# Sliding attention in a two-layer decoder trunk: the scores of both key blocks packed into one 128x128 tile per head, turned once, and put back by masked copies on VectorE

## The chip, the cores and the metric

The kernel runs on one core of one Trainium2 chip. The metric is the device time in microseconds of one execution. The kernel before took 1579.21 us (median of 3 runs, 1577.72 to 1579.51).

## What is computed

Two layers of a hybrid decoder over 512 tokens and 1024 model columns, batch 1, float32. Each layer normalises x, makes one combined input projection and feeds three branches: a short gated convolution, a gated linear attention (GLA) and a sliding-window attention. Their outputs go through branch projections, gates and an output projection, and then through an MLP of width 4096. The part that matters here is the sliding attention: window 128, blocks of 128 queries, 8 query heads over 2 key heads of width 64, a sink per head.

```python
kw = with_prev_block(k)                          # the block before and this block: 256 keys
s = einsum('bnqkgd,bnckd->bkgnqc', qb, kw)
diff = qpos[:, :, None] - kpos[:, None, :]
mask = (diff >= 0) & (diff < SWA_WINDOW) & (kpos >= 0)
s = where(mask, s, -inf)
m = maximum(max(s, axis=-1), sink)
p = exp(s - m)
denom = sum(p, axis=-1) + exp(sink - m)
o = einsum('bkgnqc,bnckd->bnqkgd', p, vw) / denom
```

A query at place q of its block sees the keys 0 to q of its own block and the keys q+1 to 127 of the block before. So of the 256 columns of a score row exactly 128 count, and each column index 0 to 127 is valid in one of the two blocks, never in both. In the first block there is no block before.

## The kernel before, in words

All weights are streamed from HBM in units. For each unit ScalarE (ACT) writes a rounded high part (`split_high`, line 885), VectorE (DVE) the remainder (`split_low`, line 1193), and TensorE (PE) multiplies with three matmuls per 128x128 piece: high by high, low by high, high by low (lines 590 to 592, 612 to 614 and 653 to 655). Each matmul moves 512 columns. A unit is 24 of them; ACT and DVE split about three units ahead of PE. `+cx1` in a table of orders stands for the split of unit cx1; `cx1` on PE for its matmuls (`cx1.0` and `cx1.1` are the halves) and on DVE for reading its result out of PSUM.

Nothing is scheduled at run time. Three tables of words, `PE_ORDER`, `ACT_ORDER` and `DVE_ORDER`, say in which order each engine does the work of the first stage of a layer; each engine works strictly in its order, and semaphores make it wait for the others. Small products (scores, transposes, attention outputs) go through four PSUM banks that are used in turn: the n-th fill waits until fill n-4 has been read.

The sliding attention has eight steps per layer: i = 0 to 7, where i // 4 is the half of the heads (four heads each) and i % 4 the block of queries. For each i, in the code from line 785 on for PE, 1021 on for ACT and 1471 on for DVE:

- `SCi` on PE: scores of 4 heads in two banks, each 2 heads x 256 keys (only 128 keys where i % 4 is 0), line 790.
- `SCi` on DVE: per bank one add of the mask into `probs` (line 1479), then the maximum over all 4 heads (line 1483) and four small operations. `SCi` on ACT: one exp per head (line 1026). `SMi` on DVE: the reciprocal of the sum; `SMi` on ACT: the scaling per head (line 1033).
- `PTi` on PE: four transposes of 128x128 for the block before (`prev`) into one bank and four for the own block (`cur`) into another (line 801); where i % 4 is 0 only the latter. `PTi` on ACT: a copy of each bank into `probs_keys` (line 1039).
- `PVi` on PE: values times probabilities, for the block before and for the own block (line 809), which waits for the copies. `PVi` on ACT and DVE: high and low part of the result (lines 1046 and 1504).

Other words that the text needs: `KV` builds the GLA states on DVE (lines 1438 and 1443), `YG` scales the GLA outputs there (line 1463), `YT` turns and splits them (lines 780 and 1469), `cc`, `ct`, `cv`, `cl` are steps of the convolution, `GO` is the GLA output, `gate` the gates, `br` the branch projections.

```python
elif kind == "PV":
    ...
    if n:
        pe.wait_ge(pprev_ready, l * 6 + half * 3 + n)
        for kv in range(SWA_KV):
            weighted(kv, 0)
    pe.wait_ge(pcur_ready, l * 8 + i + 1)
```

Of the kernel before, what the change touches and what calls it, by code (L numbers as in the profile page):

```python
# [220 lines left out]
def hybrid_trunk(nc, x, x_cols, positions, params, w_in, gla_wa2, w_branch, w_o, w_up, w_down, norms, consts, gmask, out):  # L221
# [3 lines left out]
    with ctx:  # L225
# [330 lines left out]
        def _(pe):  # L556
# [1192 lines left out]
```

## Time and profile before

| what | value |
|---|---|
| median of 3 runs | 1579.21 us |
| the profiled execution's own time | 1577.71 us |
| its span, first to last instruction | 1575.9 us |
| PE busy | 1557.0 us, 99% of the span |
| DVE busy | 1040.5 us, 66% |
| ACT busy | 771.5 us, 49% |
| mean granted clock of TensorE | 0.999 of full speed |
| the sliding attention of layer 0 | from 102.5 us (SC0) to 229 us (PV7) |
| the sliding attention of layer 1 | from 884.7 us to 1012 us |

Times within the span are counted in microseconds from its start. The rows of PE give a matmul's duration from its issue to the end of its results (about 0.39 us for 512 columns), while the next one begins 0.23 us after it; what PE's time costs is therefore read from one start to the next, not from the durations.

### The profile page before, as it was taken

What the parts mean: (1) busy time and instruction counts of PE and PEld (TensorE: products, weight loads), DVE (VectorE), ACT (ScalarE), POOL (GpSimd) and SP (SyncE); (2) the same over time, 40 slices, a digit from 0 to 9 for tenths busy, and PEclk for the clock granted to TensorE, in tenths of its full rate; (3) what the DMA queues carried; (4) which work ended last, traced back from release to release, by engine and by line L of the source; (5) the groups of instructions that cost most, each with busy time, mean ns of one, the idle gap of its engine ahead of it and who ended that gap; (6) DMA issues with size and microseconds to landing.
All of it is one profiled execution on the core that took longest, in us unless ns stands there. A gap on an engine that the chain in (4) does not pass through costs nothing.

```text
span 1575.9 us, 21326 instructions
## 1 busy us (share of the span) xinstructions
PE 1557.0 (99%) x7488; PEld 1273.5 (81%) x7488; DVE 1040.5 (66%) x1487; ACT 771.5 (49%) x1163; POOL 106.9 (7%) x92
## 2 busy tenths in 40 slices
PE   8999999999999999999999999999999999999998
PEld 7877778888778888888787787788887888888886
DVE  5677664554776657586866777655457676665778
ACT  5657552222556464546445566432235563636362
POOL 0000000000121010111000000000002111101010
PEclk9999999999999999999999999999999999999999
DMA  7321314532596655748323212155316956666553
GB/s 236 103 81 57 95 64 147 173 107 81 131 222 140 176 138 150 172 109 208 56 84 104 82 54 81 54 172 175 107 54 151 243 115 178 143 174 135 142 125 94
DMA packets 132298, 201.48 MB, mean 128 GB/s; under 512 B 6592, under 2 KB 82912, under 8 KB 132192
## 3 DMA queue, kind: packets, MB, share of 16 engines
q1 hardware_dynamic: 107536, 153.36, 29.2%
q0 software_dynamic: 23936, 46.14, 17.6%
q8 instruction: 60, 0.98, 0.3%
q10 hardware_dynamic: 720, 0.61, 0.1%
q14 instruction: 46, 0.38, 0.1%
HBM read 170.74 MB, written 2.10 MB: 110 GB/s over the span
## 4 chain that ended last, share of the span: by engine, by line
PE 90%; DVE 6%; DVEq 1%; issue 1%; ACT 1%; DMA 0%; ACTq 0%
PE acc L590 19%; PE acc L592 19%; PE acc L591 19%; PE acc L653 6%; PE acc L655 6%; PE acc L654 6%; PE acc L612 3%; PE acc L614 3%; PE acc L613 3%; DVE wl_rows L1193 2%; DVE x_tokens L1555 1%; PE bank L790 1%; PE bank L809 1%; PE bank L801 1%; DVE ul L1212 1%
## 5 line engine op out<-in xcount | busy, mean ns | idle before, releaser
L590 PE MATMUL acc<-uh,wh 128*128 128x512 f32 x1152 | 452.8, 393 | 1.7 <-DVEq L1214 1.2
L592 PE MATMUL acc<-uh,wl 128*128 128x512 f32 x1152 | 448.7, 389 | 0.0
L591 PE MATMUL acc<-ul,wh 128*128 128x512 f32 x1152 | 448.5, 389 | 0.0
L590 PEld LDWEIGHTS acc<-uh,wh 128*128 128x128 f32 x1152 | 216.2, 188 | 54.0 <-issue 6.0
L592 PEld LDWEIGHTS acc<-uh,wl 128*128 128x128 f32 x1152 | 216.2, 188 | 45.5
L591 PEld LDWEIGHTS acc<-ul,wh 128*128 128x128 f32 x1152 | 216.3, 188 | 43.7
L1193 DVE TENSOR_TENSOR wl<-raw,wh 128x1024 fp32r<-128x1024 f32 x142 | 174.0, 1225 | 103.8 <-ACT wh L885 92.2
L885 ACT ACTIVATE wh<-raw 128x1024 fp32r<-128x1024 f32 x142 | 150.6, 1060 | 140.8 <-PE acc L592 86.9
L885 ACT ACTIVATE wh_rows<-raw_down 128x1024 fp32r<-128x1024 f32 x140 | 148.5, 1061 | 132.2 <-PE acc L655 99.9
L1193 DVE TENSOR_TENSOR wl_rows<-raw_down,wh_rows 128x1024 fp32r<-128x1024 f32 x140 | 171.5, 1225 | 24.5 <-ACT wh_rows L885 11.9
L1057 ACT ACTIVATE gate_tanh<-gate_tanh 128x512 f32<-128x512 f32 x40 | 25.3, 633 | 164.4 <-DVEq L1224 164.4
L1223 DVE TENSOR_TENSOR gate_tanh<-acc,rsqrt_rows 128x512 f32<-128x512 f32 x48 | 33.1, 691 | 109.1 <-PE acc L592 109.0
L1095 ACT ACTIVATE hidden<-acc 128x512 f32<-128x512 f32 x64 | 38.3, 599 | 123.0 <-PE acc L592 121.1
L612 PE MATMUL acc<-wh_rows,uh 128*128 128x512 f32 (+1 forms) x256 | 96.1, 376 | 1.5 <-DVE gla_k L1310 1.2
L614 PE MATMUL acc<-wl_rows,uh 128*128 128x512 f32 (+1 forms) x256 | 93.4, 365 | 0.0
L613 PE MATMUL acc<-wh_rows,ul 128*128 128x512 f32 (+1 forms) x256 | 93.3, 364 | 0.0
L1132 POOL DMA_DIRECT2D raw_down<-raw_down x20 | 24.2, 1211 | 840.1 <-DMA raw_down<-in_w_o_dram 601.4
L653 PE MATMUL acc<-wh_rows,hidden_hi 128*128 128x512 f32 x192 | 75.3, 392 | 1.1 <-DVE wl_rows L1193 1.1
L655 PE MATMUL acc<-wl_rows,hidden_hi 128*128 128x512 f32 x192 | 74.8, 389 | 0.0
L654 PE MATMUL acc<-wh_rows,hidden_lo 128*128 128x512 f32 x192 | 74.8, 389 | 0.0
L590 PE MATMUL acc<-yh,wh 128*128 128x512 f32 x192 | 74.7, 389 | 0.0
L591 PE MATMUL acc<-yl,wh 128*128 128x512 f32 x192 | 74.7, 389 | 0.0
(257 smaller groups left out, 2440.0 us busy)
## 6 DMA issues: line engine op xcount, KB each, us to landing
raw<-in_w_in_dram SPq DMA_DIRECT2D x39, 1024.0 KB, 5.2
raw<-in_w_up_dram SPq DMA_DIRECT2D x32, 1024.0 KB, 6.2
raw_down<-in_w_down_dram SPq DMA_DIRECT2D x32, 1024.0 KB, 8.6
raw_down<-raw_down POOLq DMA_DIRECT2D x44, 512.0 KB, 5.6
raw_down<-in_w_down_dram POOLq DMA_DIRECT2D x32, 512.0 KB, 6.3
raw_branch<-in_w_in_dram SPq DMA_DIRECT2D x12, 1024.0 KB, 5.0
raw_branch<-in_w_branch_dram SPq DMA_DIRECT2D x12, 1024.0 KB, 5.0
raw_down<-in_w_o_dram SPq DMA_DIRECT2D x8, 1024.0 KB, 8.2
```

Of the source, the lines that this page charges most:

```text
L590: nc.tensor.matmul(a[:], wh[slot][:, k, :], right_h, start=at_k == 0, stop=False)
L591: nc.tensor.matmul(a[:], wh[slot][:, k, :], right_l, start=False, stop=False)
L592: last = nc.tensor.matmul(a[:], wl[slot][:, k, :], right_h, start=False, stop=at_k == n - 1)
L612: nc.tensor.matmul(to, left_h[:, k, s], h[:, row, 0:cols], start=k == 0, stop=False)
L613: nc.tensor.matmul(to, left_l[:, k, s], h[:, row, 0:cols], start=False, stop=False)
L614: last = nc.tensor.matmul(to, left_h[:, k, s], lo[:, row, 0:cols], start=False, stop=k == KT - 1)
L653: nc.tensor.matmul(to[:], left[0], h[:, row, :], start=k == 0, stop=False)
L654: nc.tensor.matmul(to[:], left[1], h[:, row, :], start=False, stop=False)
L655: last = nc.tensor.matmul(to[:], left[0], lo[:, row, :], start=False, stop=k == BK - 1)
L885: nc.scalar.activation(split_view(True, u, l), raw_view(u), ACT.Copy).then_inc(hi_done, 1)
L1095: nc.scalar.activation(hid[:, k, :], a[:], ACT.Relu).then_inc(free, 1)
L1193: V.tensor_tensor(split_view(False, u, l), raw_view(u), split_view(True, u, l).bitcast(f32), ALU.subtract).then_inc(lo_done, 1)
```

## The change

In every block but the first of each half, DVE no longer adds a mask to 256 score columns per head. It copies the 128 columns of the own block into `probs` and then copies the columns of the block before over them, under a mask, where the key lies after the query. `probs` is half as wide, and so are the maximum, the exp and the scaling. PE turns one 128x128 tile per head (four transposes for every i), into one bank. Putting the turned probabilities back into the two halves of `probs_keys` is DVE's: `PTi` is now a word of `DVE_ORDER` and no longer of `ACT_ORDER`; it is one masked copy of 128x512 where i % 4 is 0, and two otherwise. Where a mask is off, `probs_keys` keeps the zeros that a new word `ptz` writes on ACT once per layer. `PVi` waits once, for both halves. Two masks more come with the GLA mask (192 KB where it was 64 KB), and the additive mask is half as wide (64 KB less).

```diff
-+gv2 sq0 sq1 sq2 sq3 ZB +gv3 KT0 +gr0 +gr1 +gr2 gv0 gv1 KT1 gv2 KD +gr3 gv3 QT0 QT1 QT2 QT3 +cx0 SC0 SM0 SC1 +cx1 PT0
-SM1 PV0 +cx2 gr0 PT1 gr1 gr2 SC2 gr3 +cx3 GO0 SC3 SM2 GO1 +cc0 SM3 PV1 PT2 mz1 +cc1 mz2 mz0 mz3 PV2 +cc2 +cc3 PT3 SC4
...
+SM1 PV0 +cx2 gr0 gr1 gr2 SC2 gr3 +cx3 GO0 SC3 SM2 GO1 +cc0 SM3 PV1 mz1 +cc1 mz2 mz0 mz3 PV2 +cc2 +cc3 SC4
...
-SC5 +cb0 YT0 +cb1 cc1 PV3 SM5 cc2 +cb2 YT1 cc3 SC6 +cb3 YT2 PV4 SM6 cv0 +gate0 YT3 ct1 SC7 cl0 ct2 SM7 PV5 cv1 cv2
-+gate1 +gate2 cl1 ct3 +gate3 PV6 cv3 cl2 +br0 cl3 gate0 PV7 gate1 +br1 gate2 +br2 gate3""".split()
...
+SC5 +cb0 YT0 +cb1 cc1 PV3 SM5 cc2 +cb2 YT1 PT4 cc3 SC6 +cb3 YT2 PV4 SM6 cv0 PT5 +gate0 YT3 ct1 SC7 cl0 ct2 SM7 PV5 cv1 cv2
++gate1 +gate2 PT6 cl1 ct3 +gate3 PV6 cv3 cl2 +br0 PT7 cl3 gate0 PV7 gate1 +br1 gate2 +br2 gate3""".split()
...
                     elif kind == "PT":
                         pe.wait_ge(probs_ready, l * 8 + i + 1)
-                        for cur in ((0, 1) if i % TT else (1,)):
-                            b = open_bank(l, word + ("cur" if cur else "prev"))
-                            for h in range(4):
-                                last = nc.tensor.transpose(b[:, h * P:(h + 1) * P], sm[i % 2][:, h, cur * P:(cur + 1) * P], ident)
-                            last.then_inc(bank_full, 1)
+                        b = open_bank(l, word)
+                        for h in range(4):
+                            last = nc.tensor.transpose(b[:, h * P:(h + 1) * P], sm[i % 2][:, h, :], ident)
+                        last.then_inc(bank_full, 1)
...
+                        pe.wait_ge(probs_T_ready, l * 8 + i + 1)
                         if n:
-                            pe.wait_ge(pprev_ready, l * 6 + half * 3 + n)
                             for kv in range(SWA_KV):
                                 weighted(kv, 0)
-                        pe.wait_ge(pcur_ready, l * 8 + i + 1)
...
-                    elif kind == "PT":
-                        for cur in ((0, 1) if i % TT else (1,)):
-                            b, free = filled(l, word + ("cur" if cur else "prev"))
-                            nc.scalar.activation(pT[:, cur].rearrange("p h c -> p (h c)"), b[:], ACT.Copy).then_inc(free, 1)
-                            nc.scalar.drain().then_inc(pcur_ready if cur else pprev_ready, 1)
+                    elif kind == "ptz":
+                        nc.scalar.activation(pT[:].rearrange("p c h n -> p (c h) n"),
+                                             zero_col.unsqueeze(2).broadcast_to([P, 2 * 4, P]), ACT.Copy).then_inc(probs_T_zero, 1)
...
-                            V.tensor_tensor(sm[buf][:, 2 * odd:2 * odd + 2, first:],
-                                            b[:].rearrange("p (j c) -> p j c", j=2)[:, :, first:],
-                                            swam.unsqueeze(1).broadcast_to([P, 2, 2 * P])[:, :, first:], ALU.add).then_inc(free, 1)
+                            to, keys = sm[buf][:, 2 * odd:2 * odd + 2, :], b[:].rearrange("p (j c) -> p j c", j=2)
+                            if i % TT:
+                                V.tensor_copy(to, keys[:, :, P:])
+                                V.drain()
+                                V.copy_predicated(to, in_block_before.unsqueeze(1).broadcast_to([P, 2, P]),
+                                                  keys[:, :, 0:P]).then_inc(free, 1)
+                            else:
+                                V.tensor_tensor(to, keys[:, :, P:], swam.unsqueeze(1).broadcast_to([P, 2, P]),
+                                                ALU.add).then_inc(free, 1)
...
+                    elif kind == "PT":
+                        b, free = filled(l, word)
+                        dve.wait_ge(probs_T_zero, l + 1)
+                        for cur in ((0, 1) if i % TT else (1,)):
+                            last = V.copy_predicated(pT[:, cur], keys_of[:, cur].unsqueeze(1).broadcast_to([P, 4, P]),
+                                                     b[:].rearrange("p (h n) -> p h n", h=4))
+                        last.then_inc(free, 1)
+                        V.drain().then_inc(probs_T_ready, 1)
```

**The order on DVE around PT6.** Before, in layer 0, this is what stands between PV5 and PV6 (`wl` rows are splits of units, here gate1, gate2 and gate3):

```order
L1504 TENSOR_TENSOR yl<-bank,yh 64x2x128 x2
L1357 TENSOR_TENSOR conv_taps_140<-acc,conv_taps_140 128x512
L1357 TENSOR_TENSOR conv_taps_139<-acc,conv_taps_139 128x512
L1193 TENSOR_TENSOR wl_63<-raw_52,wh_59 128x1024
L1193 TENSOR_TENSOR wl_64<-raw_53,wh_60 128x1024
L1229 TENSOR_TENSOR yl<-conv_taps_140,yh 128x512
```

The same place in the changed kernel:

```order
L1512 TENSOR_TENSOR yl<-bank,yh 64x2x128 x2
L1351 TENSOR_TENSOR conv_taps_140<-acc,conv_taps_140 128x512
L1351 TENSOR_TENSOR conv_taps_139<-acc,conv_taps_139 128x512
L1187 TENSOR_TENSOR wl_63<-raw_52,wh_59 128x1024
L1187 TENSOR_TENSOR wl_64<-raw_53,wh_60 128x1024
L1501 COPY_PREDICATED probs_keys<-masks,bank 128x512 x2
L1223 TENSOR_TENSOR yl<-conv_taps_140,yh 128x512
```

The two masked copies of PT6 stand behind the splits of gate1 and gate2, where before no work of the sliding attention stood.

**The order on DVE around PT0.** Before, from SM1 on (the first `gla_states` row is the start of KV1):

```order
L1493 TENSOR_TENSOR small<-small 128x4
L1495 RECIPROCAL small<-small 128x4
L1193 TENSOR_TENSOR wl_63<-raw_52,wh_59 128x1024
L1438 COPY gla_states<-bank 128x128
L1443 SCALAR_TENSOR_TENSOR gla_states<-gla_states,gla_exp_b,bank 128x128 x6
```

In the changed kernel:

```order
L1493 TENSOR_TENSOR small<-small 128x4
L1495 RECIPROCAL small<-small 128x4
L1187 TENSOR_TENSOR wl_63<-raw_52,wh_59 128x1024
L1501 COPY_PREDICATED probs_keys<-masks,bank 128x512
L1432 COPY gla_states<-bank 128x128
L1437 SCALAR_TENSOR_TENSOR gla_states<-gla_states,gla_exp_b,bank 128x128 x6
```

The one masked copy of PT0 stands between the split of cx1 and KV1.

**The order on PE around PV6.** PE's order keeps its words; in the changed kernel PT6, the rest before PV6 and PT7 are these rows of small products:

```order
L800 MATMUL bank<-consts,probs_103 128x128 x4
...
L808 MATMUL bank<-probs_keys,swa_v 64x256 x4
...
L800 MATMUL bank<-consts,probs_104 128x128 x4
```

Before, both rows of transposes read x8 (line 801), and the units between them are the same.

## Rows read from the trace of the kernel before

**Rows 1.** The page: busy time of the engines, and the chain that ended last

```profile
PE 1557.0 (99%) x7488; PEld 1273.5 (81%) x7488; DVE 1040.5 (66%) x1487; ACT 771.5 (49%) x1163; POOL 106.9 (7%) x92
PE 90%; DVE 6%; DVEq 1%; issue 1%; ACT 1%; DMA 0%; ACTq 0%
```

**Rows 2.** Busy time by stretch, late in layer 0's attention (stretch: us, each engine, clock)

```profile
200.00:210.00 10.00, 10.00 (x52) 7.70 (x51) 8.75 (x15) 5.54 (x16) 0.00 (x0) 1.00 0.00 1
210.00:220.00 10.00, 10.00 (x52) 7.69 (x51) 8.46 (x14) 7.04 (x12) 0.00 (x0) 1.00 0.33 107
```

**Rows 3.** Timeline of PE: PT0 (x4), PT2 (x8) and what follows (start, us)

```profile
112.78 0.60 PE L801 MATMUL bank<-consts,probs 128*128 128x128 f32 x4
113.14 0.47 PE L612 MATMUL acc<-wh_rows,uh 128*128 128x512 f32 x1
...
144.73 1.03 PE L801 MATMUL bank<-consts,probs 128*128 128x128 f32 x8
145.52 0.48 PE L590 MATMUL acc<-uh,wh 128*128 128x512 f32 x1
```

**Rows 4.** Timeline of DVE: masked copies of GLA, SC2 (128x512) and SC4 (128x256)

```profile
99.56 1.61 DVE L1432 COPY_PREDICATED gla_att<-gla_mask,bank 128x512 f32<-128x512 int32 x2 [0.19 <-PE bank L718]
...
124.53 1.29 DVE L1479 TENSOR_TENSOR probs<-bank,consts 128x512 f32<-128x512 f32 x2 [0.25 <-issue]
125.91 1.22 DVE L1483 TENSOR_REDUCE small<-probs 128x4 f32<-128x1024 f32 x1
...
165.01 0.75 DVE L1479 TENSOR_TENSOR probs<-bank,consts 128x256 f32<-128x256 f32 x2 [1.93 <-PE bank L790]
165.86 0.69 DVE L1483 TENSOR_REDUCE small<-probs 128x4 f32<-128x512 f32 x1
```

**Rows 5.** Groups by line: the masked copies, and ACT's copies of the turned probabilities

```profile
L1432 DVE COPY_PREDICATED gla_att<-gla_mask,bank 128x512 f32<-128x512 int32 x8 | 5.9, 738 | 1.2 <-PE bank L718 0.4 <-issue 0.2
...
L1039 ACT ACTIVATE probs_keys<-bank 128x512 f32<-128x512 f32 x28 | 16.7, 598 | 11.3 <-PE bank L801 9.0
```

**Rows 6.** Timeline of PE: the starts of PV0, PV2, PV3, PV6 and PV7, layer 0

```profile
117.08 0.65 PE L809 MATMUL bank<-probs_keys,swa_v 128*64 128x256 f32 x4
...
151.16 1.08 PE L809 MATMUL bank<-probs_keys,swa_v 128*64 128x256 f32 x8
...
167.79 1.08 PE L809 MATMUL bank<-probs_keys,swa_v 128*64 128x256 f32 x8
...
216.57 1.08 PE L809 MATMUL bank<-probs_keys,swa_v 128*64 128x256 f32 x8
...
226.92 1.08 PE L809 MATMUL bank<-probs_keys,swa_v 128*64 128x256 f32 x8
```

**Rows 7.** Timeline of DVE: what stands ahead of PT0 and PT2

```profile
116.14 1.23 DVE L1193 TENSOR_TENSOR wl<-raw,wh 128x1024 fp32r<-128x1024 f32 x1 [0.17 <-issue]
...
142.20 0.69 DVE L1341 TENSOR_TENSOR conv_u<-acc,temps 128x512 f32<-128x512 f32 x1 [4.59 <-PE acc L592]
...
147.62 2.19 DVE L1463 SCALAR_TENSOR_TENSOR gla_o<-gla_o,factors_o,gla_gate 128x128 f32<-128x128 f32 x8
```

**Rows 8.** Timeline of DVE from SC6 to the split ahead of PT7

```profile
188.97 1.29 DVE L1479 TENSOR_TENSOR probs<-bank,consts 128x512 f32<-128x512 f32 x2 [0.44 <-PE bank L790]
...
199.22 0.75 DVE L1469 SCALAR_TENSOR_TENSOR yl<-bank,params,yh 128x512 fp32r<-128x512 f32 x1 [0.73 <-ACT yh L1020]
...
215.26 1.23 DVE L1193 TENSOR_TENSOR wl<-raw,wh 128x1024 fp32r<-128x1024 f32 x1 [0.18 <-issue]
...
225.03 0.69 DVE L1193 TENSOR_TENSOR wl<-raw_branch,wh 128x512 fp32r<-128x512 f32 x1 [0.54 <-ACT wh L885]
```

**Rows 9.** Layer 1: PV6 on PE and the split ahead of it on DVE

```profile
998.78 1.08 PE L809 MATMUL bank<-probs_keys,swa_v 128*64 128x256 f32 x8
...
997.46 1.23 DVE L1193 TENSOR_TENSOR wl<-raw,wh 128x1024 fp32r<-128x1024 f32 x1 [0.18 <-issue]
```

**Rows 10.** Transfers of the first 40 us: GB/s by slice, and the masks

```profile
GB/s 0 24 151 301 351 399 399 389 393 384 357 361 389 387 364 346 348 374 385 347 255 351 360 300 308 40 11 0 0 0 8 0 0 0 0 49 233 403 399 375
gla_mask<-in_gmask_dram ACTq DMA_DIRECT2D x1, 64.0 KB, 6.6
```

More of the change, by code:

```diff
@@ L81 @@
 PE_FIRST = "gq0.0 gq1.0 gq0.1 gq1.1 gk0 gk1.0 UT0 NROW gk1.1".split()
-ACT_ORDER = """+gk1 UT0 UT1 ss0 UT2 UT3 ss1 ss2 ss3 +kva0 +kva1 attz +kva2 +kva3 +sq0 +sq1 +sq2 kva0 kva1 kva2 kva3 +sq3 +gv0 ZA +gv1
-+gv2 sq0 sq1 sq2 sq3 ZB +gv3 KT0 +gr0 +gr1 +gr2 gv0 gv1 KT1 gv2 KD +gr3 gv3 QT0 QT1 QT2 QT3 +cx0 SC0 SM0 SC1 +cx1 PT0
-SM1 PV0 +cx2 gr0 PT1 gr1 gr2 SC2 gr3 +cx3 GO0 SC3 SM2 GO1 +cc0 SM3 PV1 PT2 mz1 +cc1 mz2 mz0 mz3 PV2 +cc2 +cc3 PT3 SC4
-+cb0 YT0 PV3 SM4 +cb1 SC5 +cb2 SM5 YT1 PT4 +cb3 YT2 PV4 SC6 +gate0 PT5 YT3 SM6 cb0 PV5 +gate1 SC7 +gate2 PT6 SM7 cb1
-cb2 +gate3 PV6 PT7 +br0 cb3 gate0 PV7 +br1 gate1 +br2 gate2 gate3""".split()
+ACT_ORDER = """+gk1 UT0 UT1 ss0 UT2 UT3 ss1 ss2 ss3 +kva0 +kva1 attz +kva2 +kva3 +sq0 +sq1 +sq2 kva0 kva1 kva2 kva3 ptz +sq3 +gv0 ZA +gv1
++gv2 sq0 sq1 sq2 sq3 ZB +gv3 KT0 +gr0 +gr1 +gr2 gv0 gv1 KT1 gv2 KD +gr3 gv3 QT0 QT1 QT2 QT3 +cx0 SC0 SM0 SC1 +cx1
+SM1 PV0 +cx2 gr0 gr1 gr2 SC2 gr3 +cx3 GO0 SC3 SM2 GO1 +cc0 SM3 PV1 mz1 +cc1 mz2 mz0 mz3 PV2 +cc2 +cc3 SC4
++cb0 YT0 PV3 SM4 +cb1 SC5 +cb2 SM5 YT1 +cb3 YT2 PV4 SC6 +gate0 YT3 SM6 cb0 PV5 +gate1 SC7 +gate2 SM7 cb1
+cb2 +gate3 PV6 +br0 cb3 gate0 PV7 +br1 gate1 +br2 gate2 gate3""".split()
 DVE_ORDER = """+gk1 UT0 UT1 UT2 UT3 RN +kva0 NROW gk0 +kva1 +kva2 gk1 +kva3 +sq0 +sq1 +sq2 kva0 kva1 kva2 kva3 +sq3 AT +gv0 ZA ZB
-+gv1 sq0 sq1 sq2 sq3 +gv2 X0 +gv3 QS +gr0 QM +gr1 X1 QR +gr2 ATT0 +gr3 ATT1 SC0 +cx0 SM0 SC1 KV0 SM1 +cx1 KV1 PV0 +cx2
-gr0 SC2 gr1 gr2 SC3 gr3 +cx3 SM2 GO0 SM3 cx0 GO1 OS YG0 cx1 YG1 +cc0 +cc1 cx2 +cc2 PV1 PV2 cx3 +cc3 SC4 cc0 ct0 SM4
-SC5 +cb0 YT0 +cb1 cc1 PV3 SM5 cc2 +cb2 YT1 cc3 SC6 +cb3 YT2 PV4 SM6 cv0 +gate0 YT3 ct1 SC7 cl0 ct2 SM7 PV5 cv1 cv2
-+gate1 +gate2 cl1 ct3 +gate3 PV6 cv3 cl2 +br0 cl3 gate0 PV7 gate1 +br1 gate2 +br2 gate3""".split()
++gv1 sq0 sq1 sq2 sq3 +gv2 X0 +gv3 QS +gr0 QM +gr1 X1 QR +gr2 ATT0 +gr3 ATT1 SC0 +cx0 SM0 SC1 KV0 SM1 +cx1 PT0 KV1 PV0 +cx2
+gr0 PT1 SC2 gr1 gr2 SC3 gr3 +cx3 SM2 GO0 SM3 cx0 GO1 OS YG0 PT2 cx1 YG1 +cc0 +cc1 cx2 +cc2 PV1 PV2 cx3 +cc3 PT3 SC4 cc0 ct0 SM4
+SC5 +cb0 YT0 +cb1 cc1 PV3 SM5 cc2 +cb2 YT1 PT4 cc3 SC6 +cb3 YT2 PV4 SM6 cv0 PT5 +gate0 YT3 ct1 SC7 cl0 ct2 SM7 PV5 cv1 cv2
++gate1 +gate2 PT6 cl1 ct3 +gate3 PV6 cv3 cl2 +br0 PT7 cl3 gate0 PV7 gate1 +br1 gate2 +br2 gate3""".split()
 PE_LATE = """wo0 wo1 wo2 wo3 wo4 wo5 wo6 wo7 wo8 wo9 wo10 wo11 wo12 V0 V1 V2 V3 wo13 up0.0 V4 V5 V6 V7 up1.0 up2.0 up3.0 up0.1
@@ L274, in hybrid_trunk @@
         attm = at("gla_att", 76, [GLA_HEADS, TT, P])
-        sm = [at(f"probs{i}", 80 + 2 * i, [4, 2 * P]) for i in range(2)]
+        sm = [at(f"probs{i}", 80 + 2 * i, [4, P]) for i in range(2)]
         gt = at("gate_tanh", 80, [4, SEQ])
@@ L310, in hybrid_trunk @@
         cst = after("consts", [N_CONST])
-        gm = after("gla_mask", [P], i32)
+        masks = after("masks", [3, P], i32)
+        gm, keys_of = masks[:, 0], masks[:, 1:]
         par = after("params", [N_PARAMS])
@@ L860, in _ @@
                 act.dma_start(xc[:, k, :], x_cols[k * P:(k + 1) * P]).then_inc(xc_full[k], 16)
-            act.dma_start(gm[:], gmask).then_inc(gm_full, 16)
+            act.dma_start(masks[:].rearrange("p c n -> p (c n)"), gmask).then_inc(gm_full, 16)
             def filled(l, name):
@@ L1022, in _ @@
                         act.wait_ge(scores_ready, l * 8 + i + 1)
-                        keys = slice(0, 2 * P) if i % TT else slice(P, 2 * P)
                         buf = i % 2
                         for h in range(4):
-                            nc.scalar.activation(sm[buf][:, h, keys], sm[buf][:, h, keys], ACT.Exp,
+                            nc.scalar.activation(sm[buf][:, h, :], sm[buf][:, h, :], ACT.Exp,
                                                  bias=neg4[buf][:, h:h + 1], accum_out=sum4[buf][:, h:h + 1])
@@ L1030, in _ @@
                         act.wait_ge(den_ready, l * 8 + i + 1)
[L1031 removed]
                         for h in range(4):
[L1033 removed]
+                            last = nc.scalar.activation(sm[i % 2][:, h, :], sm[i % 2][:, h, :], ACT.Copy,
                                                         scale=den4[i % 2][:, h:h + 1])
                         last.then_inc(probs_ready, 1)
[L1036 to L1040 removed]
+                    elif kind == "ptz":
+                        nc.scalar.activation(pT[:].rearrange("p c h n -> p (c h) n"),
+                                             zero_col.unsqueeze(2).broadcast_to([P, 2 * 4, P]), ACT.Copy).then_inc(probs_T_zero, 1)
                     elif kind == "PV":
@@ L1705, in constants @@
     c[:, CC["scan"]:CC["scan"] + SEQ] = np.arange(SEQ) % GLA_CHUNK != 0
-    key = np.arange(2 * P)[None, :]
-    c[:, CC["swam"]:CC["swam"] + 2 * P] = np.where((key > p[:, None]) & (key <= p[:, None] + P), 0.0, -3.0e38)
+    c[:, CC["swam"]:CC["swam"] + P] = np.where(p[None, :] <= p[:, None], 0.0, -3.0e38)
     freq = np.float32(500000.0) ** (-np.arange(0, 2 * half, 2, dtype=np.float32) / np.float32(2 * half))
```

27 lines of the change are left out of this document (12 added, 15 removed).

## The prediction

> **What bounds the kernel now.** I read the page first: PE is busy for 99% of the span and carries 90% of the chain that ended last, so time is gained by taking instructions from PE and lost wherever PE waits [rows 1]. The busy time by stretch says how much room the others have where the change works: between 200 and 220 us DVE is busy 8.75 and 8.46 us of each 10, ACT 5.54 and 7.04, PE all of it, at full clock [rows 2]. So ACT gives up work at a place where it had room, and DVE takes it where it has little. The question is then one of due times, not of sums: each PVi on PE now waits for masked copies that stand in DVE's strict order, and I compare, from the timelines of PE and DVE, when PE reaches PVi and when DVE can have done PTi. Both layers show the same picture: PV6 starts at 216.57 and 998.78, the split ahead of it on DVE at 215.26 and 997.46, so both lie 782.2 us apart [rows 6, 8, 9]. I work out layer 0 and double it.
>
> **What PE saves.** From the start of PT0's four transposes to the next matmul PE takes 0.36 us, from the start of PT2's eight 0.79 us [rows 3]. Four transposes fewer are 0.43 us. Six of eight steps per layer have them: 6 x 0.43 x 2 layers = **-5.2 us**. This is the whole gain; the matmuls of SC and PV stay.
> The row of a transpose reads 0.27 us long, but they overlap, and only the distance of starts counts. The Trainium skill ("TensorE: Matmul & The Clock Gate", Part 4: PE-mode transpose) gives about 275 ns for a 128x128 transpose in a kernel's context; taken as the cost of each, 48 transposes fewer would be 13.2 us, and the sum below would come out 8 us lower. The starts in the trace speak against that.
>
> **What the new work costs DVE.** A masked copy of 128x512 out of PSUM takes 0.74 us [rows 5]; two in a row with a drain between take 1.61 [rows 4]. PT has no drain between its two, so I take 2 x 0.74 less the 0.03 to 0.09 by which back-to-back operations overlap (two adds of 0.69 take 1.29 [rows 4]), 1.45 us, plus 0.17 us that DVE idles ahead of each word (the small idle times in [rows 7, 8]): **1.62 us** for a pair, **0.91 us** for the single copy of PT0 and PT4. From the end to PE's start I add 0.1 us for drain and semaphore, about what separates dependent steps in the timeline.
> SC changes too. Before: two adds in 1.29 and a maximum in 1.22. After, for i % 4 not 0: two copies and two masked copies of 128x256 with a drain in each pair, and a maximum of 0.69 [rows 4]. A pair of 128x256 adds takes 0.75 [rows 4], so four such operations without drains are 1.5, with two drains (0.08 each) and somewhat slower masked copies about 1.8: +0.5 against -0.53. I take **0**. Bounds: had the four cost no more than the two adds, -0.5 per SC; had a 128x256 operation the price of a 128x512 one (0.69 and 0.74), +1.6 - 0.53 = +1.1 per SC.
>
> **Where PE waits then.**
> *PV0.* The split of cx1 ends at 116.14 + 1.23 = 117.37 [rows 7]. PT0's copy: + 0.91 = 118.28, + 0.1 = 118.38. PE is there at 117.08 [rows 6]: **1.3 us**. ACT's copy hid this before, since ACT had nothing else then.
> *PV2.* DVE resumes at 142.20 on a result of PE [rows 7], so it keeps its distance to PE. YG0 ends at 149.81; + 1.62 + 0.1 = 151.53. PE was there at 151.16 [rows 6], and PT2 is now 0.43 shorter, so 150.73: **0.8 us**.
> *PV6.* SC6 on DVE waited for PE at 188.97 [rows 8]; from there to the split of gate2 DVE is bound by its own work but for one wait of 0.73 us at 199.22 [rows 8]. PT5 puts 1.62 in; 0.56 of that wait absorbs part (0.17 stays). The split of gate2, which ended at 216.49, ends at 217.55; PT6: + 1.62 + 0.1 = 219.27. PE was at PV6 at 216.57, and PT5 and PT6 between are 0.86 shorter: 215.71. **3.56 us.** Even if PT5 cost nothing, PT6 stands behind a split that ended 0.08 us ahead of PV6.
> *PV7.* The split of br0 waits for ACT, which waits for the unit gate0 on PE; it ends at 225.03 + 0.69 = 225.72 [rows 8]. + 1.62 + 0.1 = 227.44 against 226.92 on PE [rows 6]: **0.5 us**. (DVE itself, late by the above, comes to that split at about the same moment.)
> *The others are in time.* PT3: DVE idles 1.93 us ahead of SC4 [rows 4], so its copies follow PE's transposes and end some 2 us ahead of PV3 [rows 6]; SC4 begins about 1 us later relative to PE, and the convolution behind it waits for PE anyway. PT1 has 14 us to PV1; PT4 and PT5 end 2.2 and 1.6 us ahead of PV4 and PV5 by the same working. KV1, gr0 to gr2 and SC2 and SC3 on DVE shift by up to 2.5 us behind PT0 and PT1; GO0 and GO1 on PE need the banks of SC2 and SC3 and find them free 1.4 and 2.1 us early, and the 4.59 us of idle time at 142.20 takes the rest [rows 7]. Splits are done three units (16 us) ahead of PE; delays of 2 to 4 us don't reach it.
> Sum of waits: 1.3 + 0.8 + 3.56 + 0.5 = 6.2 per layer, **+12.4 us**.
>
> **Edits that I cost at nothing.** ACT loses its 28 copies of 0.60 us [rows 5] and about 0.1 us per head in exp and scaling; nobody waits for ACT at those places but PT, whose probabilities are in time. The new zero fill on ACT (1024 columns, about 1.1 us) stands ahead of the split of sq3, 16 us before PE needs it. The masks bring 128 KB more in the first 25 us, when the transfers run at 350 to 400 GB/s [rows 10]: 0.35 us if all of it lay on the path, nothing if the loads end behind cover; I take 0 and keep 0.35 for the range.
>
> **Sum.** 1577.71 - 5.2 + 12.4 = 1584.9 us against the profiled execution's own time. The median of the runs is 1.5 us above that execution, so the same difference of +7.2 gives 1586.4; I say **1586.0 us**, slower by 0.4%. A difference below 0.2% (3.2 us) can't be told from none here.
>
> **Rivals.**
> *A, DVE's copies stay hidden; faster.* Then only the saving is left: 1579.2 - 5.2 = 1574.0. It needs DVE at PT6 3.56 us earlier than worked out, and PV0 and PV2 hidden too. For it: the other four PTs are in time, and if SC were 0.5 us shorter each, 1 us would come back at PV6 (SC6, SC7) and 0.5 at PV0. Against it: that leaves 2.5 us at PV6, and PT6's own place suffices for a wait of over 1.6 us. 5%.
> *B, about no change.* Only PV6 waits, the three small ones dissolve: -5.2 + 2 x 3.56 = +1.9, 1581.1. They rest on differences of 0.5 to 1.3 us and on my handoff and copy times. With SC at its lower bound too, it is 1579.1. 13%.
> *C, a longer wait.* SC at its upper bound puts 1.1 more ahead of PV0 and 2.2 more ahead of PV6: +6.6 in two layers, 1593. The same side as my forecast. 7%.
> *D, the clock.* PE stands still for 3.6 us twice, in a stretch in which it was always busy at full clock [rows 2]. If the granted clock fell to its lower level of 1.2 GHz behind it for as long as the wait, each would cost some 2 us more: 1590. Nothing in the trace shows such a fall. 5%.
> *E, the loads at the start* add at most 0.35; within my range.
>
> **How the numbers follow.** My forecast holds 70%. Range for 8 in 10: from 1581.0 (half of B's weight lies below) to 1591.0 (D and part of C). Faster by over 0.2% (below 1576.0) is A and a little of B: 7%. Within 0.2% (up to 1582.4) is most of B and the lower edge of the forecast: 13%. Slower: 80%.
>
> **What would show it.** Right: 64 transposes instead of 112, PE idle ahead of PV0, PV2, PV6 and PV7 with DVE's masked copies as what ended it, by 1.3, 0.8, 3.6 and 0.5 us, the same in both layers, PV6 the longest; SC on DVE about as long as before; PE's busy time down by about 5 us. Wrong: PV6 starting right behind the unit before it (then A), or a large wait elsewhere on PE, at PV3 or PV5, at GO0 (banks of SC2), or at a split that comes late.

## The result, and the profile after

| | before | after |
|---|---|---|
| median, us | 1578.60 (1577.72 to 1579.51, 4 runs) | 1591.52 (1590.77 to 1595.08, 4 runs) |
| profiled execution: time, span | 1577.71, 1575.9 | 1590.77, 1589.0 |
| mean granted clock | 0.999 | 0.997 |
| TensorE transposes of probabilities | 112 | 64 |

The ratio is 1.0083, 95% interval 1.0071 to 1.0096: slower by 0.8%, where 0.4% was forecast, and just above the range (1591.0). The page after, the lines that answer to [rows 1]:

```profile
PE 1555.6 (98%) x7440; PEld 1271.5 (80%) x7440; DVE 1057.8 (67%) x1539; ACT 746.8 (47%) x1137; POOL 106.9 (7%) x92
PE 80%; DVE 13%; DVEq 2%; issue 2%; ACT 1%; DMA 1%; SPq 0%; ACTq 0%
```

PE has 48 instructions less. Its busy time is less by only 1.4 us, though (by 5.5 us, 1551.5, in the kernel further down that has no waits and full clock), and its share of the chain fell from 90% to 80%, DVE's rose from 6% to 13%. PE's timeline has the four waits of layer 0 (start, us, what, and in brackets the idle time ahead and who ended it; L1504 is the drain behind PT's masked copies):

```profile
119.05 0.65 PE L808 MATMUL bank<-probs_keys,swa_v 128*64 128x256 f32 x4 [1.36 <-DVEq L1504]
...
153.48 0.87 PE L808 MATMUL bank<-probs_keys,swa_v 128*64 128x256 f32 x6 [1.14 <-DVEq L1504]
...
221.03 1.32 PE L808 MATMUL bank<-probs_keys,swa_v 128*64 128x256 f32 x8 [3.45 <-DVEq L1504]
222.28 0.79 PE L590 MATMUL acc<-uh,wh 128*128 128x512 f32 x1
222.87 0.63 PE L591 MATMUL acc<-ul,wh 128*128 128x512 f32 x1
223.30 0.63 PE L592 MATMUL acc<-uh,wl 128*128 128x512 f32 x1
...
225.00 0.47 PE L590 MATMUL acc<-uh,wh 128*128 128x512 f32 x1
225.31 0.39 PE L591 MATMUL acc<-ul,wh 128*128 128x512 f32 x1
...
226.46 0.60 PE L800 MATMUL bank<-consts,probs 128*128 128x128 f32 x4
...
233.31 1.05 PE L808 MATMUL bank<-probs_keys,swa_v 128*64 128x256 f32 x7 [0.78 <-DVEq L1504]
```

The rows at L808 are PV0, PV2, PV6 and PV7, the one at L800 is PT7. Layer 1 has the same four, with 1.35, 0.80, 3.75 and 0.43 us. Between PV6 and the next ordinary stretch the reader sees something new: matmuls that start 0.43 us apart, where they start 0.23 us apart ahead of it and from 225.31 on. The granted clock of these stretches, by windows (stretch: us, engines, clock, DMA share, GB/s):

```profile
210.00:220.00 10.00, 7.58 (x36) 5.94 (x34) 8.39 (x14) 5.75 (x15) 0.00 (x0) 1.00 0.07 10
...
222.00:224.00 2.00, 2.00 (x6) 1.43 (x5) 1.85 (x3) 0.76 (x2) 0.00 (x0) 0.50 0.24 89
224.00:226.00 2.00, 2.00 (x7) 1.54 (x7) 1.85 (x3) 0.00 (x0) 0.00 (x0) 0.71 0.00 0
...
1010.00:1012.00 2.00, 1.85 (x8) 0.89 (x8) 1.69 (x3) 0.00 (x0) 0.00 (x0) 0.56 0.83 316
1012.00:1014.00 2.00, 2.00 (x7) 1.62 (x6) 1.78 (x4) 0.76 (x2) 0.00 (x0) 0.59 0.00 0
```

The granted clock is at its lower level, 1.2 GHz, behind both waits for PV6 and comes back within 4 us. What it costs is read from the distance between PV6's start and PT7's start, between which both kernels do the same work: 3.91 us before (from 216.57 [rows 6] to the row below), 5.43 and 5.47 after, so 1.5 and 1.6 us in the two layers.

```profile
220.48 1.04 PE L801 MATMUL bank<-consts,probs 128*128 128x128 f32 x8
```

 The Trainium skill ("TensorE: Matmul & The Clock Gate", Part 1) gives 426.7 ns and 215.7 ns from start to start for a matmul of 512 columns at the two levels. The rows agree for the lower level (0.43 us); at the upper one this kernel needs 0.23.

DVE's side of the longest wait, from its timeline:

```profile
216.72 1.23 DVE L1187 TENSOR_TENSOR wl<-raw,wh 128x1024 fp32r<-128x1024 f32 x1 [0.18 <-issue]
218.12 1.22 DVE L1187 TENSOR_TENSOR wl<-raw,wh 128x1024 fp32r<-128x1024 f32 x1 [0.18 <-issue]
219.51 1.33 DVE L1501 COPY_PREDICATED probs_keys<-masks,bank 128x512 f32<-128x512 int32 x2 [0.16 <-issue]
```

The two splits (of gate1 and gate2) stand ahead of PT6, and PT6's two copies end at 220.84, just ahead of PV6 at 221.03. The new SC1 on DVE, in the same view, answers to SC in [rows 4]:

```profile
109.55 0.42 DVE L1475 COPY probs<-bank 128x256 f32<-128x256 f32 x1 [0.39 <-PE bank L790]
110.04 0.45 DVE L1477 COPY_PREDICATED probs<-consts,bank 128x256 f32<-128x256 int32 x1
110.39 0.41 DVE L1475 COPY probs<-bank 128x256 f32<-128x256 f32 x1
110.87 0.45 DVE L1477 COPY_PREDICATED probs<-consts,bank 128x256 f32<-128x256 int32 x1
111.41 0.69 DVE L1483 TENSOR_REDUCE small<-probs 128x4 f32<-128x512 f32 x1
```

From 109.55 to the maximum's end are 2.55 us; two adds and a maximum took 2.60 [rows 4]. SC costs DVE nothing, as taken.

**Where the 13.06 us between the profiled executions went**, each read from starts on PE:

| term | predicted | measured |
|---|---|---|
| 48 transposes fewer | -5.2 | -5.2 to -5.5 (each four 0.43 to 0.48) |
| waits ahead of PV0, PV2, PV6, PV7, both layers | +12.4 | +13.06 |
| clock at its lower level behind PV6 | 0 (a rival, 5%) | +3.1 |
| start, up to SC0 | 0, up to 0.35 | +0.54 (102.49 to 103.03) |
| between the layers (753 to 872 us) | 0 | +1.1 |

The last one comes in three steps of about 0.36 us (PE's lateness goes from 6.38 to 7.48 us). That sum is 12.3 to 12.6. Part of the rest lies where PE takes up work again: its lateness grows by 1.43 us at both PV0 where the wait's row says 1.36 and 1.35.

### The profile page after: what moved, and what is told of

The parts are those of the page before. It is cut to its first block, busy times and chain, and to the rows that moved or that the text cites. A ratio compares the mean times of both kernels' runs of the same rounds, so it can differ in the third digit from the quotient of the medians.

```text
span 1589.0 us, 21286 instructions
## 1 busy us (share of the span) xinstructions
PE 1555.6 (98%) x7440; PEld 1271.5 (80%) x7440; DVE 1057.8 (67%) x1539; ACT 746.8 (47%) x1137; POOL 106.9 (7%) x92
## 4 chain that ended last, share of the span: by engine, by line
PE 80%; DVE 13%; DVEq 2%; issue 2%; ACT 1%; DMA 1%; SPq 0%; ACTq 0%
PE acc L590 17%; PE acc L592 17%; PE acc L591 17%; PE acc L653 6%; PE acc L655 6%; PE acc L654 6%; PE acc L612 3%; PE acc L614 3%; PE acc L613 3%; DVE wl_rows L1187 3%; DVE x_tokens L1563 1%; DVE wl L1187 1%; PE bank L790 1%; PE bank L808 1%; DMA raw<-in_w_in_dram 1%
## 5 line engine op out<-in xcount | busy, mean ns | idle before, releaser
L1187 DVE TENSOR_TENSOR wl_rows<-raw_down,wh_rows 128x1024 fp32r<-128x1024 f32 x140 | 171.5, 1225 | 25.3 <-ACT wh_rows L883 12.4
```

Source lines behind the costliest of these rows:

```text
L1187: V.tensor_tensor(split_view(False, u, l), raw_view(u), split_view(True, u, l).bitcast(f32), ALU.subtract).then_inc(lo_done, 1)
```

## The experiments

All kernels ran beside the kernel before on the same chip; its medians there were 1579.45, 1579.42 and 1579.28 us. Four theories were to be told apart, of which the first three can hold together. T1: waits add up, and the clock's fall belongs to the wait for PV6. T2: the late start is the additional mask transfer's. T3: the three steps between the layers are stalls of DVE's own instruction stream. T4, the rival to all: time is lost by something else in the change (more work on DVE, ACT's zero fill). Where a text below says what the lower clock cost, it is read as above, from the distance of the same two starts on PE in two traces.

**One slot earlier for PT6.** One split instead of two ahead of it.

```diff
-+gate1 +gate2 PT6 cl1
++gate1 PT6 +gate2 cl1
```

> The changed kernel (profiled at 1590.8 us) with PT6 on VectorE one split earlier, between +gate1 and +gate2. Both theories: the masked copies end one split (1.4 us) earlier, so PE's wait ahead of PV6 is 3.45 - 1.4 = about 2.1 us in layer 0 and 2.4 in layer 1. Theory W+C (it is the long wait that makes the clock fall, and a wait of some 2 us doesn't): no matmul behind PV6 at the lower clock, the start-to-start distance from PV6 to PT7 back at 3.9 us from 5.4, 1590.8 - 2 x 1.4 - 2 x 1.5 = 1585.0. Rival W (the fall of the clock has another cause and stays, or any wait of this size brings it): 1588.0, with some matmuls behind PV6 still 0.43 us apart.

1589.63 us (1588.25 to 1591.06), ratio 1.0071 [1.0057, 1.0085]; my theory, that a wait of some 2 us leaves the clock alone, gave 1585.0, the rival 1588.0. PV6's wait in layer 0, and the clock behind it in both layers:

```profile
219.22 1.72 PE L808 MATMUL bank<-probs_keys,swa_v 128*64 128x256 f32 x8 [2.11 <-DVEq L1504]
...
220.00:222.00 2.00, 2.00 (x9) 1.06 (x6) 1.74 (x4) 0.76 (x2) 0.00 (x0) 0.50 1.02 393
...
1008.00:1010.00 2.00, 2.00 (x7) 1.62 (x6) 1.74 (x4) 0.76 (x2) 0.00 (x0) 0.50 0.89 342
```

The wait is shorter by one split, as said, but the clock falls behind waits of 2.11 and 2.41 us as well, and costs the same: 5.45 us from PV6 to PT7 in layer 0. The rival was right. A shorter wait isn't a safe one.

**PT6 ahead of both splits.**

```diff
-+gate1 +gate2 PT6 cl1
+PT6 +gate1 +gate2 cl1
```

> The changed kernel with PT6 on VectorE two splits earlier, ahead of +gate1. The copies end 2.8 us earlier: PE waits 0.65 us ahead of PV6 in layer 0 and 0.95 in layer 1. Theory W+C: full clock throughout, 1590.8 - 2 x 2.8 - 2 x 1.5 = 1582.2. Rival W: 1585.2 with the lower clock still there. PV7's wait stays at 0.4 to 0.8 in both, since the split of br0 ahead of it waits for PE's own unit gate0.

1594.75 us (1592.25 to 1596.59), ratio 1.0098 [1.0084, 1.0112], where 1582.2 or 1585.2 was expected: no gain at all.

```profile
218.27 1.08 PE L808 MATMUL bank<-probs_keys,swa_v 128*64 128x256 f32 x8 [0.72 <-DVEq L1504]
...
231.71 1.97 PE L808 MATMUL bank<-probs_keys,swa_v 128*64 128x256 f32 x8 [3.48 <-DVEq L1504]
...
1010.02 1.08 PE L808 MATMUL bank<-probs_keys,swa_v 128*64 128x256 f32 x8 [1.02 <-DVEq L1504]
...
1023.11 1.98 PE L808 MATMUL bank<-probs_keys,swa_v 128*64 128x256 f32 x8 [3.13 <-DVEq L1504]
...
234.00:236.00 2.00, 2.00 (x6) 1.52 (x6) 0.84 (x2) 0.72 (x2) 0.00 (x0) 0.50 0.00 0
```

PV6 now waits 0.72 us, PV7 3.48: together 4.20, as 3.45 + 0.78 = 4.23 in the changed kernel. My expectation that PV7's wait is fixed by gate0 fell. PE reached PV7 at 228.23 instead of 232.53, 4.3 us sooner, but PT7's copies started only 1.6 us sooner (230.19 against 231.78): in the changed kernel DVE idled 1.65 us ahead of the split of br0, here it idled nowhere there, and its own work set the time. The clock falls at PV7 instead of behind PV6 (0.50 from 234 to 236 and from 1025 to 1027), and it costs more there: the lower level lasts until 237.4, over 5 us of PE's work, and PE loses 2.6 us in layer 0 and 2.9 in layer 1, where the changed kernel lost 1.5 and 1.6. In this execution it also falls behind both old waits of 2.3 us (near 442 and 1234, 1.6 and 1.5 us; of them more below). So this kernel is no faster than the changed one although its waits at PV6 and PV7 have the same sum. Moving one late copy moved the wait.

**All four copies early.**

```diff
-KV0 SM1 +cx1 PT0 KV1
+KV0 PT0 SM1 +cx1 KV1
-OS YG0 PT2 cx1
+OS PT2 YG0 cx1
-SM7 PV5 cv1 cv2
+SM7 PT6 PV5 cv1 cv2
-+gate1 +gate2 PT6 cl1 ct3 +gate3
++gate1 +gate2 cl1 ct3 PT7 +gate3
-+br0 PT7 cl3
++br0 cl3
```

> All four late masked copies moved ahead on VectorE: PT0 ahead of SM1, PT2 ahead of YG0, PT6 ahead of PV5, PT7 ahead of +gate3. If the order of these words is the whole cause (my theory), PE waits at no PV, the clock is full, and the saving of 48 transposes comes through: 1577.7 - 5.2 + 0.5 (later loads at the start) = 1573.0, up to 1574.0 with the 1.0 us that went between the layers. Rival (VectorE has no room: the waits only move to other words, to GO0, SC banks or late splits): 1577 or more, with waits on PE of over 0.5 us elsewhere.

1575.40 us (1574.89 to 1578.47, 11 runs), ratio 0.9980 [0.9972, 0.9989]: faster than before, if by 0.2%, and 1.4 to 2.4 us above the 1573.0 to 1574.0 expected. All four waits are gone, and the clock's fall with them:

```profile
100.00:240.00 140.00, 139.51 (x794) 109.36 (x793) 105.84 (x217) 69.02 (x169) 0.00 (x0) 1.00 0.22 69
```

DVE does the same work, 1057.6 us in all against 1057.8 in the changed kernel, and ACT's zero fill is there too. So neither was the cause (T4 falls), only the place of four of DVE's words. One new wait of 0.48 us (0.60 in layer 1) stands at SC3, a product near 1174 us starts another 0.35 late, and these are most of what the expectation lacked:

```profile
127.20 0.49 PE L790 MATMUL bank<-swa_k,swa_q 64*128 64x256 f32 x2 [0.48 <-DVE probs_keys L1501]
```

**Two of the four each.** To add up the parts, only PT6 and PT7 were moved in one kernel, only PT0 and PT2 in another, each by its lines of the diff above.

> The changed kernel with PT6 and PT7 alone moved forward on VectorE (PT6 ahead of PV5, PT7 ahead of the split of gate3); PT0 and PT2 stand where the change put them. If the wait and the clock behind it add up as read from the trace, this takes back 2 x (3.6 + 0.6) of waits and 2 x 1.5 of clock, 11.4 us: 1580.1 against 1591.5. If the clock had nothing to do with the waits, the fall stays and it is 1583.1. The two waits of 1.36 and 1.14 us ahead of PV0 and PV2 stay, and behind them the clock stays at its upper level.

1580.65 us (1579.00 to 1582.47, 11 runs), ratio 1.0009 [1.0000, 1.0018]. That is 10.9 us below the changed kernel's 1591.5, where the sum with the clock says 11.4 and the sum without it 8.4. With four runs of the changed kernel the medians alone hardly tell these two apart; PE's starts do. From PV6 to PT7 it is 3.91 us again, as before the change. The waits of 1.35 and 1.14 us stay, and the clock stays up behind them:

```profile
217.30 1.08 PE L808 MATMUL bank<-probs_keys,swa_v 128*64 128x256 f32 x8
...
221.21 0.60 PE L800 MATMUL bank<-consts,probs 128*128 128x128 f32 x4
...
153.27 1.08 PE L808 MATMUL bank<-probs_keys,swa_v 128*64 128x256 f32 x8 [1.14 <-DVEq L1504]
...
118.00:122.00 4.00, 3.16 (x15) 2.39 (x16) 2.95 (x8) 0.76 (x2) 0.00 (x0) 1.00 0.79 251
153.00:157.00 4.00, 3.73 (x20) 2.84 (x21) 3.56 (x11) 1.72 (x3) 0.00 (x0) 1.00 0.00 0
```

> The changed kernel with PT0 and PT2 alone moved forward on VectorE. The waits ahead of PV0 and PV2 go (1.36 + 1.14 and 1.35 + 0.80, 4.65 us in all), the waits ahead of PV6 (3.5 to 3.8 us) and PV7 stay, with the clock's fall behind both: 1591.5 - 4.7 = 1586.8. Rival: TensorE, earlier by 2.3 us at SC6, finds VectorE as late as before, so that the gain is lost again at PV6, whose wait grows to 4.5 us or more: 1589 to 1591.

1588.99 us (1587.01 to 1590.49, 5 runs), ratio 1.0063 [1.0050, 1.0075], against 1586.8 expected; profiled 1587.01, 3.8 below the changed kernel's profiled 1590.77.

```profile
126.91 1.13 PE L790 MATMUL bank<-swa_k,swa_q 64*128 64x256 f32 x8 [0.46 <-DVE probs_keys L1501]
...
218.35 1.76 PE L808 MATMUL bank<-probs_keys,swa_v 128*64 128x256 f32 x8 [3.45 <-DVEq L1504]
```

The four waits at PV0 and PV2 (4.65 us) are gone, SC3's two new ones (0.46 and 0.59) give 1.05 back: 3.6. PV6's wait is 3.45 as it was, so the rival, that it would grow, is refuted: DVE's work from SC6 on follows PE and came sooner with it. The median is higher than the profiled time, and so is the part of the time at the lower clock in those runs (mean clock 0.995 in the longest two, 0.997 in the shortest).

**SC3's wait.** PT1 one word forward in the kernel with four early.

```diff
-gr0 PT1 SC2 gr1
+PT1 gr0 SC2 gr1
```

> The kernel with the four copies early, and PT1 one word further forward on VectorE, ahead of the split of gr0. With the four early, TensorE waits 0.48 and 0.60 us at SC3, whose second bank is PT1's and is free only when VectorE has copied PT1 out. If that is what it waits for, both waits go, since PT1's copies end 1.3 us sooner, and it is 1.1 us faster: 1573.8 for the fastest run against 1574.9. Rival: SC2, which now comes right behind, holds the wait (its bank is freed by the same engine no earlier), and nothing is gained.

1575.81 us (1574.30 to 1577.39, 9 runs), ratio 0.9980 [0.9970, 0.9989]. Both waits at SC3 are gone, and PE is 0.55 us earlier from there on in layer 0, 0.68 in layer 1. The fastest runs differ by 0.6 us (1574.30 to 1574.89), where 1.1 was expected, and the ratios not at all. The clock goes with it: the mean clock is 1.000 in 5 of 11 runs of the kernel with four early, in 2 of 9 of this one, and these alone differ by 0.9 us in their means (1575.32 and 1574.44). In the profiled one it fell behind an old wait at 432.15, which took back 1.6 us between 433 and 436.

**The load at the start.** The kernel before, plus the mask's additional 128 KB into a tile that nobody reads.

```diff
-            act.dma_start(gm[:], gmask).then_inc(gm_full, 16)
+            act.dma_start(gm[:], gmask[:, 0:P]).then_inc(gm_full, 16)
+            act.dma_start(unread[:], gmask[:, P:]).then_inc(gm_full, 16)
```

> The kernel before, plus the one transfer of the change: its larger mask table (the 128 KB more) is loaded on the same queue into a tile that nobody reads. If the transfer alone delays the start, SC0's scores start some 0.5 us later on TensorE than the 102.49 of before (at 102.9 to 103.1), ACT's wait for the first weights grows from 3.55 to about 3.95 us, and all later distances stay; whole time +0.5. If the delay came from the new zero fill on ACT or from anything else of the change, SC0 stays at 102.5 and the time too. In both cases the four waits ahead of PV0, PV2, PV6 and PV7 are absent.

1579.83 us (1577.89 to 1581.81, 11 runs), ratio 1.0003 [0.9995, 1.0012]. The whole time doesn't resolve 0.4 us; ACT's timeline does. The wait for the first large weights, before, after, and here:

```profile
18.16 2.26 ACT L885 ACTIVATE wh<-raw 128x1024 fp32r<-128x1024 f32 x2 [3.55 <-DMA raw<-in_w_in_dram]
```

```profile
18.93 1.06 ACT L883 ACTIVATE wh<-raw 128x1024 fp32r<-128x1024 f32 x1 [3.96 <-DMA raw<-in_w_in_dram]
```

```profile
19.23 1.06 ACT L887 ACTIVATE wh<-raw 128x1024 fp32r<-128x1024 f32 x1 [3.97 <-DMA raw<-in_w_in_dram]
```

The transfer alone brings the 0.4 us in ACT's wait. SC0 came at 103.29, later than said. One trace is not enough for it, though: in the eight traces of kernels that load the three masks at once, SC0 starts anywhere from 102.43 to 103.03.

**The masks late.** The other way round, with the four early: only the first mask goes ahead, the two new ones stand behind the scan mask on SyncE's queue.

```diff
-            act.dma_start(masks[:].rearrange("p c n -> p (c n)"), gmask).then_inc(gm_full, 16)
+            act.dma_start(masks[:, 0], gmask[:, 0:P]).then_inc(gm_full, 16)
...
+                    sp.dma_start(masks[:, 1:].rearrange("p c n -> p (c n)"), gmask[:, P:]).then_inc(masks_full, 16)
...
-            dve.wait_ge(masks_full, 16)
+            dve.wait_ge(masks_full, 32)
```

> e3 with the two new masks loaded apart, by the queue of the weights behind the scan mask, so that the first loads are as large as before. Theory (the 128 KB delay the weights of gk0 by 0.8 us, and with them the norm factors that PE waits for at 36 us): the first SC0 on PE is back at 102.5 us from 103.0, and the time 0.5 us below e3. Rival (the shift comes from the zero fill ptz or another source): no difference to e3 within 0.1 us in the start of SC0.

1576.63 us (1574.86 to 1579.94, 11 runs), ratio 0.9984 [0.9976, 0.9993]. SC0 starts at 102.28, against 102.70 with the masks early: the 0.4 us is back. The whole time doesn't show it (fastest 1574.86 and 1574.89). Over all twelve traces, SC0 starts at 102.35 in the mean where the first loads are small (the kernel before, this one and the last one below) and at 102.80 where they are large (the other nine), and ACT's wait is 3.55 to 3.68 us against 3.81 to 3.97. So T2 holds, for 0.4 us in the mean; the 0.54 of the changed kernel's one trace has some chance in it.

**The stream of DVE's instructions.** The steps between the layers start at DVE, with idle time in which it waits for nothing that the trace shows. In the changed kernel:

```profile
759.39 1.23 DVE L1187 TENSOR_TENSOR wl_rows<-raw_down,wh_rows 128x1024 fp32r<-128x1024 f32 x1 [0.44 <-issue]
...
815.69 0.16 DVE L1234 SCALAR_TENSOR_TENSOR stat<-stat,rsqrt_tokens 128x4 f32<-128x4 f32 x1 [0.43 <-issue]
...
872.09 0.20 DVE L1232 TENSOR_TENSOR stat<-squares_qk,factors_qk 128x40 f32<-128x40 f32 x1 [0.43 <-issue]
```

Where the kernel before does the same operations, there is no such gap:

```profile
752.65 1.23 DVE L1193 TENSOR_TENSOR wl_rows<-raw_down,wh_rows 128x1024 fp32r<-128x1024 f32 x1
...
808.58 0.16 DVE L1240 SCALAR_TENSOR_TENSOR stat<-stat,rsqrt_tokens 128x4 f32<-128x4 f32 x1
```

The changed DVE program has more instructions (1539 busy ones against 1487). T3 was tried with 24 instructions more, put into 8.9 us of idle time.

```diff
                     elif kind == "df":
+                        if l == 0 and i == 2:
+                            for _ in range(24):
+                                V.drain()
                         dve.wait_ge(hid_val, (l * QUARTERS + i) * 8 + BK)
```

> The kernel with all four copies early, plus 24 drains on VectorE in layer 0 ahead of the third subtraction of the feed-forward's differences, where VectorE idles 8.9 us. Theory: the three steps of 0.35 us that the changed kernel loses between the layers are stalls of VectorE's own instruction stream (0.43 to 0.45 us idle with nothing to wait for, at 751.1, 807.4 and 863.8 of the kernel with the copies early), whose place is set by how many instructions stand ahead, so that they move by 24 instructions: out of the two chains of small operations into places where VectorE waits anyway. Then TensorE's idle 0.41 ahead of the down projection's matmul and 0.35 ahead of the row factors go, and it is 0.7 to 1.05 us faster than the kernel with the copies early (1574.9 fastest). Rival: the stalls belong to those operations or to ACT's zero fill; they stay where they are, and the time too.

1576.84 us (1573.90 to 1578.07, 11 runs), ratio 0.9983 [0.9974, 0.9991]. The same operation without the drains, and with them:

```profile
807.40 0.16 DVE L1234 SCALAR_TENSOR_TENSOR stat<-stat,rsqrt_tokens 128x4 f32<-128x4 f32 x1 [0.43 <-issue]
...
809.73 0.29 PE L678 MATMUL bank<-consts,rsqrt_tokens 128*128 128x128 f32 x1 [0.35 <-DVEq L1362]
```

```profile
806.76 0.16 DVE L1234 SCALAR_TENSOR_TENSOR stat<-stat,rsqrt_tokens 128x4 f32<-128x4 f32 x1
...
809.09 0.29 PE L678 MATMUL bank<-consts,rsqrt_tokens 128*128 128x128 f32 x1
```

All three stalls left these places, and between 778 and 916 us PE gained 1.0 us; the gaps ahead of these stayed where they were (at 312 and 598 us). The fastest run is 1.0 us faster (1573.90 to 1574.89), though the median is 1.4 us slower, again with the clock: 3 of 11 runs at 1.000 against 5 of 11. T3 holds for the places and their price.

The traces say more of the places than this one run. Number all of DVE's records in the order of their starts, from 0, with those that the page doesn't count (drains, semaphores). In each of the twelve traces, every idle time of 0.40 to 0.45 us that neither the record before nor a semaphore explains stands ahead of a record whose number is 63 more than a multiple of 128: 319, 447, 831, 1087, 1215, 1471 and 2111 are the first in the kernel before, and the three stalls above are records 1599, 1727 and 1855 of the changed one. Not every such record has one. With the 24 drains, 1599 and the others fall on other instructions, as said. Which process makes such a stall was not tried.

**All together.** Four copies and PT1 early, masks late, and the drains; the diffs above in one kernel.

> All that helped, together: the four copies and PT1 early, the two new masks loaded behind the others on SyncE's queue, and the 24 drains of before. Fastest run of the kernel with the four early 1574.9, less 1.1 (SC3's two waits), less 0.4 (start), less 1.0 (three stalls of VectorE's stream): 1572.4; its median against the kernel before 0.996 to 0.997. If the small terms hide each other, no more than 1 us of them shows: 1573.9. TensorE's clock is at its upper level but for what may fall behind the old waits of 2.3 us at about 432 and 1213 us, which costs up to 1.6 us each in any of these kernels.

1576.12 us (1574.21 to 1576.95, 11 runs), ratio 0.9977 [0.9968, 0.9986]: no different from the kernel with the four early alone, and the fastest run is 1.8 us above the 1572.4 expected. In PE's starts the first terms are there (the old wait ends at 431.77 against 432.72, 0.95 us earlier), but no run had a clock of 1.000, and the profiled one has the lower clock behind both old waits:

```profile
1212.00:1220.00 8.00, 6.76 (x23) 5.51 (x24) 5.81 (x5) 4.41 (x5) 4.88 (x4) 0.79 0.91 149
430.00:438.00 8.00, 6.23 (x21) 5.08 (x22) 5.78 (x6) 4.33 (x6) 4.89 (x4) 0.79 0.88 149
```

In the profiled run of the kernel before, the same stretches:

```profile
430.00:438.00 8.00, 5.68 (x26) 4.41 (x25) 7.39 (x7) 5.42 (x7) 2.78 (x3) 1.00 0.89 151
1212.00:1220.00 8.00, 5.68 (x26) 4.40 (x25) 7.39 (x7) 5.40 (x7) 2.61 (x3) 1.00 0.88 150
```

Read from PE's starts against the kernel with the four early, which kept full clock there, the two falls cost 1.5 us each, 3.1 of the profiled 1575.69: an estimate of some 1572.6 without them, against the expected 1572.4. No run measured that. Why the clock falls there in some executions and in others not stays open; these waits stood in the kernel before the change too.

## Why the prediction was right and wrong

**Right: the direction and the waits.** What the prediction read as due times came out: 1.3, 0.8, 3.56 and 0.5 us per layer were forecast; 1.36, 1.14, 3.45, 0.78 were found in layer 0 and 1.35, 0.80, 3.75, 0.43 in layer 1. The saving was 0.43 to 0.48 us for four transposes. With the 275 ns that the Trainium skill ("TensorE: Matmul & The Clock Gate", Part 4) gives for one, of bf16, the sum would have been 8 us lower; the trace does not agree with it as a distance of starts (0.11 to 0.12 us for each of these in float32). SC on DVE cost nothing, the pair of masked copies 1.33 to 1.36 us (1.45 taken), and PV1 and PV3 to PV5 wait for nothing. That rival A and B fell follows from the same rows: none of the four waits dissolved, though the two short ones rested on differences of about 1 us. C, SC at its upper bound, fell with SC's rows.

**Wrong: the clock, a term left at zero.** The step that failed is "nothing in the trace shows such a fall", by which rival D got 5%. The trace of before couldn't show it at this place, because PE had no wait there; I priced the waits as if PE came back at full speed. It measured +3.1 us, three quarters of D's price (some 2 us each; 1.5 and 1.6 found). The kernel with PT6 and PT7 early shows it from the other side: with the two waits gone, PV6 to PT7 is 3.91 us again. The other sign that failed, PE's busy time down by about 5 us, failed with it: it came down by 1.4, and by 5.5 where the clock stayed up. And the profiled execution before had PE idle for 2.3 us near 434 and 1217 us at full clock, while other executions of the same kernel took 1.4 to 3.7 us more, at a mean clock of 0.997 to 0.999; the prediction rested on the one.

**Wrong in small terms, all of one sign.** The additional mask load was taken as hidden, with 0.35 kept; SC0 came 0.54 late, 0.4 of which is the load's. Three stalls of DVE's stream cost 1.1, a term that I hadn't got at all, and whose place goes by how many instructions stand ahead. The waits were 0.66 longer in sum, and restarts cost a little more than their rows. 3.1 + 0.54 + 1.1 + 0.66 = 5.4, the missing 5.9 us nearly.

**Right in kind, not tested by the forecast.** "DVE's strict order" was the mechanism: with the words moved, the same change is 0.2% faster than before. The working said of PV7 that DVE's own lateness "comes to that split at about the same moment" as ACT's half; the run with PT6 ahead of both splits shows that this coincidence carried PV7's small wait, which became 3.48 us once PE arrived sooner.

## What to carry to other kernels

When work moves to an in-order engine, list for each moved piece when its reader is due and what stands ahead of it; one late piece costs all of the saving, and moving that piece alone may only hand the wait to the next one, so move the group and run it. Price a wait on a TensorE that was busy as the wait plus the clock behind it (here 1.5 to 1.6 us behind 2.1 to 3.8, and up to 2.9 in one kernel), and look at several executions' mean clocks before calling a short gap free. A gain of one microsecond in a kernel of 1.6 ms is to be read from starts in the trace, since the clock behind unrelated waits moves the whole time by more.

## What the runs showed of the hardware

- The granted clock stayed at its upper level behind waits of 0.35 to 1.36 us and behind the 1.5 us near 785 that all twelve traces have. It fell at each of the eight waits of 2.11 to 3.75 us ahead of PV6 and PV7, and behind 8 of the 24 old ones of 2.3 us.
- Such a fall cost 1.5 to 1.6 us of PE's time in 14 of 16 cases, whether the wait had been 2.11 or 3.75 us, and 2.6 and 2.9 us at PV7 in the kernel with PT6 ahead, where the lower level lasted longer.
- DVE's instruction stream has stalls of 0.40 to 0.45 us, all of them 128 records apart or a multiple of it; 24 drains took three of them off the path for 1.0 us.
- A masked copy of 128x512 out of PSUM into SBUF takes 0.73 us, of 128x256 0.45, and a plain copy of 128x256 0.42.
